# Prompt attention with its two head groups in two runs, and two weight pieces loaded between cache loads

## What is computed

```
# fox:  p = softmax(q k^T * scale + c_q - c_k, causal);            out = p v
# diff: p = softmax(q1 k1^T) - lam * softmax(q2 k2^T), by chunks;  out = rms(p v) * gain
o = concat(o_fox, o_diff) @ w_out
h = x + o
# top-4 of 32 experts, each: clamped SwiGLU of (1024 -> 2048), then (1024 -> 1024)
y = h + moe(rms(h))
```

## Time and profile before

| what | value |
|---|---|
| median of 3 runs | 1271.49 us |
| the profiled execution's own time | 1270.83 us |
| span of that execution in the profile | 1269.0 us |
| TensorE busy | 1213.5 us (96%) |
| VectorE, ScalarE, GpSimd busy | 354.9, 197.6, 158.4 us |
| prompt attention | from about 162 to 202 us of the span |
| sample attention | to about 267 us |
| output projection and routing | to about 326 us |
| expert stage | to the end |

### The profile page before, as it was taken

The page is one execution under the profiler, slowest core; times in us unless marked ns, Lnnn a source line. Parts: engine busy times, 40 slices in busy tenths (PEclk is TensorE's granted clock), DMA queues, the critical chain, the costliest instruction groups (busy, mean ns, idle before and its releaser), DMA issues.

```text
span 1269.0 us, 16164 instructions
## 1 busy us (share of the span) xinstructions
PE 1213.5 (96%) x6079; PEld 535.3 (42%) x6080; DVE 354.9 (28%) x947; ACT 197.6 (16%) x523; POOL 158.4 (12%) x378
## 2 busy tenths in 40 slices
PE   7999988999899999999999999999999999999997
PEld 4444345645553434434343434344343434343432
DVE  2234366623321313212121314131221212130412
ACT  3211265423210101001010101010010101010100
POOL 0031312200401202020201202020202021020000
PEclk9999999999899999999999999999999999999998
DMA  8713522781599999999999999999999999999993
GB/s 274 273 45 115 202 98 100 260 347 38 200 429 427 427 427 428 429 429 429 428 428 428 429 429 429 427 429 429 428 429 429 429 428 428 429 428 429 427 428 163
DMA packets 55049, 447.53 MB, mean 353 GB/s; under 512 B 11089, under 2 KB 11490, under 8 KB 30434
## 3 DMA queue, kind: packets, MB, share of 16 engines
q1 hardware_dynamic: 54400, 446.87, 84.8%
q10 hardware_dynamic: 610, 0.14, 0.0%
HBM read 442.13 MB, written 4.86 MB: 352 GB/s over the span
## 4 chain that ended last, share of the span: by engine, by line
PE 66%; DMA 26%; issue 3%; DVE 2%; ACT 1%; POOL 1%; SPq 1%; POOLq 0%; ACTq 0%; DVEq 0%
DMA arena<-in_w_gate_up 25%; PE psum L1800 18%; PE psum L1768 17%; PE psum L1505 9%; PE psum L1749 7%; PE psum L1671 3%; PE psum L1815 2%; PE psum L1783 1%; PE psum L1779 1%; DMA arena<-in_w_in 1%; PE psum L1542 1%; PE psum L1572 1%; PE psum L1639 1%; PE psum L1601 1%; PE psum L1481 1%
## 5 line engine op out<-in xcount | busy, mean ns | idle before, releaser
L1768 PE MATMUL psum<-arena 128*64 128x512 f32 x2048 | 450.5, 599 | 19.0 <-DMA arena<-in_w_gate_up 18.5
L1768 PEld LDWEIGHTS psum<-arena 128*64 128x64 f32 x2048 | 152.9, 138 | 314.7 <-issue 314.7
L1800 PE MATMUL psum<-arena 128*64 128x512 f32 x1024 | 224.7, 597 | 0.8
L1365 DVE TENSOR_SCALAR arena<-psum 128x256 f32<-128x256 f32 x64 | 26.7, 418 | 432.5 <-PE psum L1768 430.7
L1800 PEld LDWEIGHTS psum<-arena 128*64 128x64 f32 x1024 | 78.8, 138 | 136.0 <-issue 134.7
L1505 PE MATMUL psum<-arena 128*128 128x512 f32 x288 | 129.0, 602 | 3.9 <-DMA arena<-in_w_in 3.3
L933 ACT ACTIVATE arena<-arena 128x256 f32<-128x256 f32 x64 | 26.7, 417 | 630.6 <-DVE arena L1365 630.6
L654 POOL COPY arena<-arena 128x6 f32 (+1 forms) x16 | 3.0, 188 | 758.2 <-PE psum L1800 703.1
L1749 PEld LDWEIGHTS psum<-arena 128*128 128x128 f32 x768 | 88.6, 194 | 16.1 <-issue 16.1
L1749 PE MATMUL psum<-arena 128*128 128x128 f32 x768 | 91.6, 279 | 3.8 <-POOL arena L661 3.8
L1815 PE MATMUL psum<-arena 128*128 128x512 f32 x192 | 93.2, 623 | 0.0
(11 more groups left out here) (239 smaller groups left out, 785.9 us busy)
## 6 DMA issues: line engine op xcount, KB each, us to landing
arena<-in_w_gate_up SPq DMA_DIRECT2D x128, 2048.0 KB, 24.9
arena<-in_w_down SPq DMA_DIRECT2D x64, 2048.0 KB, 22.6
arena<-in_w_in SPq DMA_DIRECT2D x5, 2048.0 KB, 14.4
arena<-in_cache_fox_k SPq DMA_DIRECT2D x8, 512.0 KB, 3.6
arena<-in_cache_diff_k SPq DMA_DIRECT2D x8, 512.0 KB, 4.6
arena<-in_cache_fox_v SPq DMA_DIRECT2D x8, 512.0 KB, 4.0
arena<-in_cache_diff_v SPq DMA_DIRECT2D x8, 512.0 KB, 6.0
arena<-in_w_out SPq DMA_DIRECT2D x4, 1024.0 KB, 7.1
```

The costliest lines, as they stand in the source:

```text
L1768: last = mm(banks[n][half], XT[u][:, k, half], piece_slot(s[x])[:, c0:c0 + 512], start=False, stop=(k == 7), skip_group_check=True)
L1800: last = mm(banks[hf][half], actT[:, 4 * i + c, half], w, start=False, stop=(i == 1 and c == 3), skip_group_check=True)
```

## The change

The prompt's steps are listed with g as the slowest index: all eight fox steps (F0, F1, four times) and then all eight diff steps (D0, D1, four times). The loads of slots 5 and 3 move from behind SP's loop into it: slot 5 behind the value loads of b = 4 (batch 2), slot 3 behind those of b = 5 (batch 3). No instruction of any engine is added or left out; the order numbers that waits use (`rows_no`, `rms_no`, `copies`, `copy_no`) are worked out from the list.

```
@@ -321,7 +321,7 @@
         att = [dict(where="p", g=g, j=j, qt=qt, nk=META + P * (qt + 1))
-               for j in range(4) for qt in range(2) for g in range(2)]
+               for g in range(2) for j in range(4) for qt in range(2)]
         NP = len(att)
@@ -504,8 +504,9 @@
                     sp.wait_ge(mixed, NP + 2 * (b - 4) + 2)
                     load_cache(b - 2, "v")
                     load_v3(b - 2)
-            for s in (3, 5):
-                sp.dma_start(piece_slot(s), piece_src(0, s - LEAD)).then_inc(ring_in[s], 16)
+                if b in (4, 5):
+                    s = {4: 5, 5: 3}[b]
+                    sp.dma_start(piece_slot(s), piece_src(0, s - LEAD)).then_inc(ring_in[s], 16)
             sp.wait_ge(scored, NA)
```

## The result

| | before | after |
|---|---|---|
| median | 1271.79 us (4 runs, 1270.83 to 1275.84) | 1289.72 us (4 runs, 1286.04 to 1295.47) |
| profiled execution, own time / span | 1270.83 / 1269.0 us | 1290.47 / 1288.7 us |
| mean granted TensorE clock of it | 0.986 | 0.972 |
| first L1542 of the samples' stage (L1543 after) | 201.75 | 207.24 |
| output projection starts | 267.03 | 283.88 |

What follows compares the result with a forecast made beforehand. The expert stage's DMA stream runs at its limit and starts when PE arrives, so attention time decides. 1270.83 + 1.9 (order) + 1.9 (pieces) + 0 = 1274.6; with 0.66 to the median, 1275.3 us, range 1270.0 to 1279.5.

Steps and rivals of the forecast that it cites:

- The end follows PE's arrival at the expert stage: Expert stage: its DMA stream runs at its limit, so whatever moves PE's arrival moves the end by as much.
- The fox run, 5.07 us a pair: Prompt attention, fox steps: two steps take 5.07 us in the new order, as in the old, so nothing is gained.
- The rival of a fast fox run: Prompt attention: fox steps go at PE's own pace, four pairs gain 4.3 us, giving 1269.1 us; chance 0.08.
- The diff run, 5.99: Prompt attention, diff steps: turn_out waits behind norms in every step, so two take 5.99 us instead of 5.07.
- The order, +1.9: Prompt's steps: the new order costs 1.9 us by the samples' steady pace; bounds 0 and 3.8.
- The pieces, +1.9: Samples' stage: two pieces among the cache loads delay keys 6 and values 4, costing 1.9 us; bounds 0 and 9.8.
- the sum of the queue: Samples' stage: the gapless load queue from keys 4 to values 4 takes 28.4 us from 219.3, ending at 247.7.
- pieces at the cache loads' pace: Samples' stage: pieces move at 355 GB/s, 5.9 us each, so two cost 2.0 more, giving 1277.3 us; chance 0.10.
- the rule of the Trainium skill: HBM loads: a core's share of about 358 GB/s binds, making a piece 5.9 us and the pieces' cost 3.9.
- One piece is absorbed: Samples' stage: piece 5 alone fits the queue, with keys 5 landing at about 233.5 and values 3 at about 237.
- The old place of the pieces is worth nothing: Behind SP's loop, before the residual rows: removing the pieces there gains 0, with -1.0 as the bound.
- The two terms add: Attention: SP's issues move with a PE made 1.9 us later, so the order's and pieces' costs add.

Runs made afterwards that it cites:

- e12: Changed kernel with slot 3's piece behind b = 7 and four unused unit transposes in iterations 8 to 13; median 1278.81 us, ratio 1.0002 to the kernel before.
- e1: Kernel before with only the new order of the prompt's steps, both pieces still behind SP's loop; median 1280.99 us, ratio 1.0013.
- e3: Kernel before with the new order alone, plus six unused unit transposes ahead of turn_out in iterations 8 to 13; median 1277.58 us, ratio 0.9956.
- e2: Kernel before in its old order, with only the two pieces moved among the cache loads; median 1279.2 us, ratio 1.0001.
- e4: Kernel before in its old order, with only slot 5's piece moved among the cache loads; median 1287.73 us, ratio 1.0039.
- e10: Kernel before in its old order, slot 5's piece behind the value loads of b = 4, slot 3's behind b = 7; median 1280.16 us, ratio 0.9997.
- e5: The changed kernel measured once more beside the kernel before; median 1285.92 us, ratio 1.0061.
- e6: Changed kernel with six unused unit transposes ahead of turn_out in iterations 8 to 13; median 1284.93 us, ratio 1.006.
- e7: Changed kernel with slot 3's piece loaded behind the values of b = 7 instead of b = 5; median 1281.68 us, ratio 1.0034.

## Why the prediction was wrong

**The step that failed** is the one that is not in the working: every duration was taken from a trace in which attention ran at full clock, and the sum assumes that it stays so. I walked the diff run to 5.99 us a pair with PE waiting in each step, and asked only what the wait costs by itself. My own text had PE with "only 4.0 us of work" for two fox steps of 5.07. I did not ask what TensorE's clock makes of an engine that stands still for nearly 1 us in every 3. The answer is a mean clock of 0.973 (the mean of the 19 executions) instead of the 0.986 of the kernel before's profile, 0.013 x 800 = 10 us by the fit, and 9 to 10 us by the trace of the changed kernel. The miss of the forecast is 14.4 us (1289.7 for 1275.3), so this step is the larger part of it and the size of the pieces' term the next.

Without the clock the prediction is nearer, and too low: +3.8 us was forecast. The fit has after at 1278.3 to 1278.5 against 1273.6 to 1274.1, 4.2 to 4.9 us; the trace has 16.85 - 0.64 (the later start) - 9.2 to 10.3 = 5.9 to 7.0. Point by point:

- *The end follows PE's arrival at the expert stage.* Right. From the first refill to the end the span has 926.3 us before and 927.8 after, 926.0 in e12.
- *The fox run, 5.07 us a pair.* Right: 5.14 in the changed kernel. The rival of a fast fox run is out.
- *The diff run, 5.99.* Right in its mechanism, 5.81 in size (e1 and e3), released by L1184 as forecast. One detail was wrong: in e1 L1184 waited for POOL once more (0.46 us at 194.59).
- *The order, +1.9.* The sum over iterations 8 to 14 is exact (16.97 for 17.0), but iteration 8 began at 187.40 in e1 instead of 185.9. The fit gives the whole term as 0.4 us alone (e1) and 1278.3 - 1277.2 = 1.1 beside the pieces. The traces give more. These are the prompt's first scores and the sixth L1542 of the samples' stage, in the kernel before and then in e3, which is at 1.00 all through attention:

```profile
162.39 0.52 PE L1560 MATMUL psum<-arena 64*128 64x144 f32 x4 [0.32 <-ACT arena L757]
...
221.04 1.04 PE L1542 MATMUL psum<-arena 128*128 128x128 f32 x8
```

```profile
163.32 0.52 PE L1560 MATMUL psum<-arena 64*128 64x144 f32 x4 [0.32 <-ACT arena L757]
...
225.34 1.04 PE L1542 MATMUL psum<-arena 128*128 128x128 f32 x8
```

From the first scores to the first L1542 it is 39.36 us before and 42.36 in e3, 41.3 without the 1.1 of the fill: 1.9 later, where 1.2 to 1.3 was forecast. To the sixth it is 58.65 and 62.02, 2.3 without the fill, for a term of 1.9. (The prediction's 8.0 us of VectorE in a period of 10.13 is 7.7 in the trace; nothing hangs on it.) So the term is about right, 0.4 too low, and the fit's 0.4 is too small. Its common slope takes 0.31 us off for each us at half clock wherever it lies; e1's two falls in attention cost about 2.4 us for 10.2 (0.5 up to iteration 8 and 1.9 from the first to the third L1542, beside e3), 0.24 for each.
- *The pieces, +1.9.* Right in place, mis-sized: 3.5 us at equal clock, 3.7 at the projection. By the sum of the queue, keys 6 should have landed at 247.7 - 3.1 (values 4 behind them) = 244.6; they landed at 246.1, and the values' small load at 249.7 instead of 248.1. The queue was full and moved 384 GB/s from 219.3 to 246.1 in e2, near the rate that the sum has in it (three batches of 2.16 MB and two pieces of 2.097 in 28.4 us: 376). So the bytes were right, and the landings came behind them. e2's trace has each landing: the last keys of batch 4 land 0.5 us later than in the sum (222.9 for 222.4), piece 5 1.9 later (232.3 for 230.4), keys 5 1.5 (235.0 for 233.5), piece 3 1.8 (243.3 for 241.5), keys 6 1.5. The lag comes with the first piece and does not grow, which speaks against a slower rate. By 246.1 the queue had moved 384 x 26.8 = 10.3 MB, while all that was issued up to keys 6 is 9.6 MB: an estimate, by which part of values 4 was moved before keys 6 had landed. The sum had each load land before the next one moves. The rival "pieces at the cache loads' pace" gives the right size (3.9) with a rate that the trace does not show: 384, not 355. The same holds for the rule of the Trainium skill that I had set beside it ("DMA: Bandwidth & Descriptors", Where 436 GB/s comes from).
- *One piece is absorbed.* Right (e4), and two are too when they stand apart (e10).
- *The old place of the pieces is worth nothing.* Right: PE's wait for L1233 in the output projection is again 0.97 us at 299.07.
- *The two terms add.* About right without the clock: by the fit 0.4 + 3.5 = 3.9, and together 4.2 to 4.9; by the traces 2.3 + 3.7 = 6.0, and together 5.9 to 7.0. In measured ratios they don't: each half alone gives 1.001 and 1.000, both together 1.006 and 1.013 (the intervals of e1 and e2 reach to 1.006 and 1.005). It is the clock that does not add. e2 has 6 of 10 executions at 0.985 or more, the whole change none of 31.

**How large the effect is** depends on the kernel before as well. In the first batch all four of its executions were at 1270.8 to 1275.8; later 56 of 106 had a clock of 0.981 or less, and its median was 1276 to 1280. The two batches put the change at 1.0061 and at 1.0128. My range was built on three executions of a program in which 56 of 106 later executions had a mean clock of 0.981 or less, and on one profile in which it had not fallen in attention.

The Trainium skill has a sentence for what happened here: "TensorE: Matmul & The Clock Gate" (section A second HAM failure mode: psum-queue depth-cycling) tells of a kernel in which TensorE idles for short moments between groups of matmuls and the clock swings between its two levels. The waits of 0.76 to 0.94 us in e1's rows and the fall behind them agree. Its section HAM oscillation — how this bites in real kernels takes half of the time at the lower level as the loss; that would be 16.5 us for the 33 here, an estimate from the page, where the trace has 9.2 to 10.3: PE waited part of the time anyway.

**What stays open.** Why the clock falls in one execution of the same kernel and not in another; what brings it down around 164 to 172, where e1, e5 and after have a fall and e3, e6, e7 and e12 with the same instructions have none; the bad batch of e4, where the old order fell too; and whether the wait of 2 us for keys brings the clock down.

## What to carry to other kernels

A reordering that leaves all work in place can still cost TensorE its clock: where it makes the engine wait shortly but in every step, price the stretch behind it at the lower level too, here 0.2 to 0.3 us for each us at half clock, and take that as a case with a chance of its own. To find out whether a slowdown is waits or clock, fill the waits with work that nobody reads and look at clock and time together: if the clock stays up and the time falls although there is more work, it was the clock. And read several executions' clocks before a range is built on a median of three.

## What the runs showed of the hardware

- The kernel before ran at 1270.4 to 1291.7 us, unchanged, and TensorE's mean clock (0.963 to 0.989) goes with nearly all of it: -8.0 us per 0.01, with 1.5 us left over. Fitted to its 106 executions alone, the slope is -8.0 too.
- With both pieces in the queue, SP's issue of a 32 KB load took 3.39 us instead of 0.47 (e2 at 237.03, 3.14 in the changed kernel at 245.81). Here it cost little: the next keys went out at 240.99 instead of the 240.63 of the kernel before, since SP would have waited for PE until then. The kernel before has one longer issue too, 1.39 us at 233.56. What holds the issue up no run shows.
- In a queue that stays full, a load's landing came 1.5 to 1.9 us behind the sum of the bytes ahead of it, at every load from the first piece on (e2).
- Full work does not bring the clock back soon. In the changed kernel PE is busy 16.8 of the 17 us from 196 to 213, all at 0.50. In e7 it is busy 10.00 of 10 from 210 to 220 and again from 220 to 230, still at 0.50 in both, and at 0.91 only in the stretch after that.
